# Where VectorE reads the decay sums and the queries in the recurrent heads, and the order of TensorE's work around two heads

## The reference, cut to what matters

```python
q, f_pre, i_v, g_o, u_a, u_b, gate_a, gate_b = jnp.split(proj, SPLITS, axis=-1)
logf = jax.nn.log_sigmoid(zf) + jnp.log1p(lb * jnp.exp(-zf))
k = (1.0 - lb) * jax.nn.sigmoid(-zf)
qh = heads(q) * (A_DK ** -0.5)
...
b = jnp.cumsum(logf, axis=2)
decay = jnp.exp(jnp.minimum(diff, 0.0)) * causal      # diff = b[t] - b[s]
attn = jnp.einsum('bhtd,bhsd,bhtsd->bhts', q, k, decay)
o = (jnp.einsum('bhts,bhsv->bhtv', attn, v)
     + jnp.einsum('bhtd,bhdv->bhtv', q * jnp.exp(b), S))
k_dec = k * jnp.exp(b_last - b)
```

## Time and profile before

| | |
|---|---|
| median of 3 runs | 852.73 us (850.11 to 853.77) |
| the profiled execution | 853.36 us |
| its span in the trace | 851.1 us |
| busy: TensorE | 811.1 us, 95% |
| VectorE | 405.9 us, 48% |
| ScalarE | 233.0 us, 27% |
| GpSimd | 141.5 us, 17% |
| bytes moved | 251.33 MB, mean 295 GB/s |

### The profile page before, as it was taken

One profiled execution on the slowest core, in us unless ns is written; L12 is line 12 of the kernel. 1 busy time (PEld: TensorE's weight loads), 2 busy tenths in 40 slices (PEclk: granted clock), 3 DMA queues, 4 the chain that ended last, 5 costly groups with the idle time before them and its releaser, 6 DMA issues.

```text
span 851.1 us, 12448 instructions
## 1 busy us (share of the span) xinstructions
PE 811.1 (95%) x5068; PEld 525.1 (62%) x5068; DVE 405.9 (48%) x682; ACT 233.0 (27%) x373; POOL 141.5 (17%) x170
## 2 busy tenths in 40 slices
PE   4999999999999999999999999999999999998892
PEld 2989999999999977585353533535335353352251
DVE  6789999988999723875011212112021120210127
ACT  6666655665444360111102010010000100000011
POOL 1354555433777200000000000000000000000000
PEclk9999999999999999999999999999999999999996
DMA  8422222344446453669999999999999999999971
GB/s 319 169 85 85 85 85 85 109 179 156 149 151 240 205 198 149 267 239 389 432 394 424 428 427 424 428 428 425 427 427 428 424 429 427 428 424 429 428 325 64
DMA packets 33894, 251.33 MB, mean 295 GB/s; under 512 B 4974, under 2 KB 8430, under 8 KB 21674
## 3 DMA queue, kind: packets, MB, share of 16 engines
q1 hardware_dynamic: 31296, 249.18, 71.8%
q10 hardware_dynamic: 2538, 1.32, 0.5%
HBM read 247.99 MB, written 2.48 MB: 294 GB/s over the span
## 4 chain that ended last, share of the span: by engine, by line
PE 69%; DVE 11%; DMA 9%; ACT 8%; issue 1%; ACTq 1%; DVEq 0%
PE ps L543 67%; DMA ring<-in_w_up_e 8%; DVE ring L1692 4%; ACT ring L1212 2%; ACT ar L1222 1%; DVE ar L1728 1%; ACT split_w L1131 1%; DVE ar L1739 1%; PE ps L940 1%; DVE ar L1683 1%; ACTq L1261 1%; ACT ar L1184 1%; DVE ring L1601 1%; DVE ar L1735 1%; ACT ar L1183 0%
## 5 line engine op out<-in xcount | busy, mean ns | idle before, releaser
L543 PE MATMUL ps<-ring,ar 128*64 128x512 f32 (+1 forms) x976 | 202.1, 567 | 1.6 <-DMA ring<-in_w_up_e 1.2
L543 PE MATMUL ps<-ring,xT 128*64 128x512 f32 (+2 forms) x848 | 151.0, 455 | 6.1 <-DMA ring<-in_w_gate_e 3.1
L543 PEld LDWEIGHTS ps<-ring,ar 128*64 128x64 f32 x976 | 67.9, 137 | 121.1 <-issue 111.8
L543 PEld LDWEIGHTS ps<-ring,xT 128*64 128x64 f32 (+1 forms) x848 | 75.5, 154 | 74.3 <-issue 63.8
L543 PE MATMUL ps<-split_x,split_t 128*128 128x320 f32 x672 | 99.2, 309 | 0.0
L543 PEld LDWEIGHTS ps<-split_x,split_t 128*128 128x128 f32 x672 | 98.6, 188 | 0.2
L2105 DVE TENSOR_TENSOR ar<-ar,ps 128x512 f32<-128x512 f32 (+1 forms) x42 | 28.7, 684 | 135.0 <-PE ps L543 134.3
L543 PE MATMUL ps<-split_x,split_w 128*128 128x320 f32 x480 | 79.8, 322 | 3.8 <-DVE split_w L1652 1.2
L543 PEld LDWEIGHTS ps<-split_x,split_w 128*128 128x128 f32 x480 | 73.2, 193 | 7.0 <-ACT split_x L1166 2.1
L1815 DVE SCALAR_TENSOR_TENSOR ps<-ar,params,ps 128x350 f32<-128x350 f32 x116 | 68.1, 587 | 4.1
L543 PE MATMUL ps<-ar 128*64 128x512 f32 (+7 forms) x424 | 66.8, 342 | 0.0
(11 more groups left out here) (232 smaller groups left out, 850.3 us busy)
## 6 DMA issues: line engine op xcount, KB each, us to landing
ring<-in_w_gate_e SPq DMA_DIRECT2D x29, 2048.0 KB, 21.8
ring<-in_w_up_e SPq DMA_DIRECT2D x29, 2048.0 KB, 18.6
ring<-in_w_down_e SPq DMA_DIRECT2D x22, 2048.0 KB, 18.1
ring<-in_w_in SPq DMA_DIRECT2D x56, 512.0 KB, 4.5
ar<-in_w_down_e SPq DMA_DIRECT2D x4, 1792.0 KB, 18.9
ring<-in_w_down_end SPq DMA_DIRECT2D x3, 2048.0 KB, 36.7
ar<-in_w_up_e SPq DMA_DIRECT2D x3, 1792.0 KB, 14.8
ring<-in_w_o_a SPq DMA_DIRECT2D x8, 512.0 KB, 5.8
```

Source lines behind the costliest of these rows:

```text
L543: return pe.matmul(out, lhsT, rhs, start=start, stop=stop)
```

## The change

VectorE's `level_decay` takes the running sum of its own columns from PSUM. Bank 0, where F(n) stood, is free by then, and a new ScalarE copy, `sum_copy`, puts `hb` there (semaphore `b_ps`). The middle value that is subtracted still comes from SBUF. `query_side` and the `hqeb` product take Q(n) straight from bank 1 in place of ScalarE's copy `hq`; the copy stays for the levels' diagonal. So QSCALE moves from that copy into the split weights: ScalarE's `w_high` scales the Q weights, VectorE's `w_low` becomes one scalar_tensor_tensor for Q. Since the banks are in use for longer, F waits for `dr_ready` (the decays of the head before) in place of `ls_ready`, and Q for `qeb_ready` in place of `q_sb`.

In TensorE's order the second head takes the levels of head 0 right behind F(1), ahead of the transposes and of Q(1). Behind the last head the levels of head 7 come right behind `conv_value(0)`, ahead of the router's matmul and `rms`.

```diff
             def cur_f(i, b, first):
...
-                    pe.wait_ge(h["ls_ready"], 2 * i + b)
+                    pe.wait_ge(h["dr_ready"], 2 * i + b)
...
             def cur_q(i, b, first):
...
-                    pe.wait_ge(h["q_sb"], 2 * i + b)
+                    pe.wait_ge(h["qeb_ready"], 2 * i + b)
...
-                if first or first_prev:
+                if first:
                     cur_q(*cur, first)
                 if first_prev:
+                    levels(*prev, True)
                     prev_kT(*prev, True)
-                    levels(*prev, True)
+                    cur_q(*cur, first)
                     prev_states(*prev)
...
-            pe.wait_ge(h["ls_ready"], 8)
+            pe.wait_ge(h["dr_ready"], 8)
             conv_value(0)
-            pe.wait_ge(h["q_sb"], 8)
+            levels(3, 1, False)
+            pe.wait_ge(h["qeb_ready"], 8)
             for k in range(KT):
                 mm(ps[:, 1, T:T + 2 * NE], ones, wgb[:, k, :], k == 0, k == KT - 1)
             rms(3, 0, 1)
-            levels(3, 1, False)
             prev_kT(3, 1, False)
...
-                signal(act, act.activation(piece(wh, q), sh[:, b, q].rearrange("p k n -> p (k n)"), ACT.Copy), whi_ready, 2 * n + q + 1)
+                signal(act, act.activation(piece(wh, q), sh[:, b, q].rearrange("p k n -> p (k n)"), ACT.Copy, scale=(1.0, QSCALE)[q]), whi_ready, 2 * n + q + 1)
...
-                signal(act, act.activation(hq[:, b, :], ps[:, 1, 0:T], ACT.Copy, scale=QSCALE), h["q_sb"], n + 1)
+                signal(act, act.activation(hq[:, b, :], ps[:, 1, 0:T], ACT.Copy), h["q_sb"], n + 1)
...
+            def sum_copy(i, b):
+
+                n = 2 * i + b
+                act.wait_ge(h["b_ready"], n + 1)
+                signal(act, act.activation(ps[:, 0, 0:T], hb, ACT.Copy), h["b_ps"], n + 1)
...
                 key_exp(*cur)
+                if first_prev:
+                    sum_copy(*cur)
                 if prev:
                     prev_states(*prev, first_prev)
+                if not first_prev:
+                    sum_copy(*cur)
                 if nxt:
                     w_high(*nxt, 0)
...
-                signal(dve, dve.tensor_tensor(piece(wl, q), sh[:, b, q].rearrange("p k n -> p (k n)"), piece(whF, q), ALU.subtract), wlo_ready, 2 * n + q + 1)
+                raw = sh[:, b, q].rearrange("p k n -> p (k n)")
+                ins = dve.scalar_tensor_tensor(piece(wl, q), raw, QSCALE, piece(whF, q), ALU.mult, ALU.subtract) if q else dve.tensor_tensor(piece(wl, q), raw, piece(whF, q), ALU.subtract)
+                signal(dve, ins, wlo_ready, 2 * n + q + 1)
...
             def level_decay(i, b):
...
+                dve.wait_ge(h["b_ps"], n + 1)
...
-                    ins = dve.tensor_tensor(xv[:, :, hs:2 * hs], bv[:, :, hs:2 * hs], bv[:, :, hs - 1:hs].to_broadcast([P, w // (2 * hs), hs]), ALU.subtract)
+                    here = ps[:, 0, 0:w].rearrange("p (m s) -> p m s", s=2 * hs)[:, :, hs:2 * hs]
+                    ins = dve.tensor_tensor(xv[:, :, hs:2 * hs], here, bv[:, :, hs - 1:hs].to_broadcast([P, w // (2 * hs), hs]), ALU.subtract)
...
-                    qv = hq[:, b, 0:w].rearrange("p (m s) -> p m s", s=2 * hs)[:, :, hs:2 * hs]
-                    ins = dve.tensor_tensor(xv, xv, qv, ALU.mult)
+                    qv = ps[:, 1, 0:w].rearrange("p (m s) -> p m s", s=2 * hs)[:, :, hs:2 * hs]
+                    ins = dve.tensor_tensor(xv, qv, xv, ALU.mult)
...
-                signal(dve, dve.tensor_tensor(hqeb, heb, hq[:, b, :], ALU.mult), h["qeb_ready"], n + 1)
+                signal(dve, dve.tensor_tensor(hqeb, ps[:, 1, 0:T], heb, ALU.mult), h["qeb_ready"], n + 1)
```

More of the change, by code:

```diff
@@ L269, in build @@
                  "kde_ready xr_ready xk_ready a_done am_ready as_ready qeb_ready kdec_ready kT_done kT_sb s_done sa_sb o_done "
-                 "osq_ready rms_done rstd_ready rstd_exp o_out so_ready so_stored hc_dve hp_dve hc_act hp_act hc_pool hp_pool fold_ready v_sb round")
+                 "osq_ready rms_done rstd_ready rstd_exp o_out so_ready so_stored hc_dve hp_dve hc_act hp_act hc_pool hp_pool fold_ready v_sb b_ps round")
         h = {n: sem(n) for n in names.split()}
```

## The result

The changed kernel takes 852.73 us (median of 20 runs, 850.96 to 855.85) against 850.99 (20 runs of the kernel before, 849.09 to 853.77): a ratio of 1.0022, 95% interval 1.0013 to 1.0031, 1.7 us slower. I had forecast 1.2 us faster. The size is inside the range and inside "within 0.5%", the direction is wrong. (The 20 runs put the kernel before at 850.99; the three that I had gave 852.73.) That 852.73 lies inside 849.0 to 854.5 says little for the working: the kernel before lies inside it too.

A forecast was written before the change was run, and what follows sets the result against it. In the steady heads a ScalarE-VectorE loop of 19.24 us was taken as the bound, TensorE 0.2 us behind. First heads +0.7, steady heads -0.98, last head -0.9 gave -1.2 us: 851.5 us, range 849.0 to 854.5.

The forecast's parts named there:

- The decays at 2.5: VectorE's seven decay subtractions in a steady head fall from 4.15 to 2.5 us with one input in PSUM.
- The ceiling of the steady heads: Five steady heads: TensorE's work, 19.06 us, replaces the 19.24 us ScalarE-VectorE loop; about 1 us gain at most.
- The 0.77 at the first `rms`: TensorE's lost 0.58 + 0.19 us up to the first `rms` vanishes, as ScalarE's chain there starts earlier.
- F-to-`rms` at 3.6: Sign of being right: TensorE goes from F's start to `rms` in 3.6 us in all heads.
- That it passes on: Behind the heads, VectorE's tap chain and TensorE both move by 1.2 us, and expert loads start 1.2 earlier.
- B: Rival: strided PSUM reads are slow, decays up to 6.0 us, 13 us more, 865; chance 0.07.
- C: Rival: VectorE and GpSimd still take turns, decays stay 4.15 and the five waits stay; 853.0, chance 0.08.
- The first heads: First two heads: TensorE idles 1.7 us before the levels, V is 1.5 late; net loss 0.7 us (0.5 to 1.2).
- GpSimd's key side speeds up only to about 3.8: Head 0: GpSimd's key side falls from 4.27 to about 3.8 us (bounds 3.6 and 4.27), ending at 41.1.
- The big exponential stays at 35.16: Head 0: ScalarE's big exponential keeps its start, released by GpSimd's decays of 3.63 us from 31.42.
- The last head: Behind the last head: levels moved ahead cover TensorE's wait for `rms`; gain 0.9 us.
- D: Rival: stages behind the heads shift VectorE's taps by 1 to 2 us, up to 853.5; chance 0.15 for over 1 us loss.

The follow-up runs named there:

- e5: The kernel before with only the two new TensorE orders (second head, last head), Q still waiting for `q_sb`; ratio 1.0003.
- e4: The changed kernel, but in head 0 VectorE's `w_low` waits until GpSimd's decays are done; ratio 0.9995.
- e3: The changed kernel with twelve extra unread matmuls into an unused bank ahead of the second head's levels; ratio 0.9995.
- e7: The kernel before with only the decays read from PSUM, and that from the second head on; head 0 reads SBUF without copy; ratio 0.9951.
- e2: The changed kernel with TensorE's old order behind the last head (router matmuls, `rms`, then levels); ratio 1.0009.
- e6: The kernel before with only `sum_copy`, F waiting for `dr_ready` and decays from PSUM in all heads; 848.90 us against 852.25, ratio 0.9952.
- e10: The same kernel as e7, run again against the kernel before; ratio 0.9966.
- e1: The changed kernel with TensorE's old order in the second head (F, Q, transposes, levels); ratio 1.0007.
- e8: The changed kernel with the old order behind the last head and head 0's `w_low` waiting for GpSimd's decays; ratio 0.9983.
- e9: The changed kernel with both old TensorE orders and head 0 as before (SBUF reads, no copy, Q(1) waiting for `q_sb`); ratio 0.9965.

## Why the prediction was wrong

**Right.** The decays at 2.5 (2.44). The ceiling of the steady heads: "TensorE sets the period at 19.06", gain 0.98; measured 18.99 and 1.28. The extra 0.06 a head is the `rms` matmuls themselves, which took 0.71 to the next start where they had been waited for (78.25 to 78.96) and take 0.63 now, less the 0.02 by which F-to-`rms` is over the 3.61 that I took. The 0.77 at the first `rms`: 0.81. F-to-`rms` at 3.6: 3.63. That it passes on, as far as the rows go: from the gates to the first expert matmul the two differ by 0.2 us, and +1.83 in the heads stands beside +1.74 between the medians; behind that matmul single executions scatter too much to tell. Rivals B and C are out: 324 ns an operation with an input in PSUM, at each stride. By the Trainium skill ("VectorE: DVE Perf Modes", the section on the TRN2 errata) a PSUM source has 62 fixed cycles more; the runs don't show that: `hqeb` with one input from PSUM (41.35 above) and the sum of two SBUF rows are both 0.49, the decays 0.324 and 0.33.

**Wrong, and it decides: the step "The first heads", with a loss of 0.7 us.** Place and releaser were right (TensorE idle ahead of the levels, GpSimd's key side the last). Every size was too small; measured from V(0) to V(1), 1.5 became 3.98. Since V(0) shifts, I take the shares from the start of VectorE's running sum of head 0 to V(1):

| kernel | sum starts | V(1) starts | between |
|---|---|---|---|
| before | 30.45 | 47.63 | 17.18 |
| e5 orders alone | 31.30 | 50.32 | 19.02 |
| e4 low part waits | 31.01 | 50.20 | 19.19 |
| e3 gap filled | 30.82 | 50.78 | 19.96 |
| changed | 30.66 | 51.82 | 21.16 |

- The order itself: I expected that filling less of the gap costs 1.5. By e5 it costs 1.84, with no read or wait changed in the heads.
- "GpSimd's key side speeds up only to about 3.8". It doesn't speed up: 4.40, and 4.24 to 4.58 in e4 to e7. Operations of 160 columns take 0.53 there (median) both before and after; I had taken the decays' 0.45 for it. The turns had cost VectorE time, 4.35 to 2.44, and GpSimd nearly none. VectorE's own gain doesn't help either, since the levels wait for the later of the two: from e5 to e4 the query side gets shorter, the key side 0.34 longer, and V(1) comes 0.17 later.
- "The big exponential stays at 35.16, because GpSimd's decays, 3.63 from 31.42, release it". They didn't stay 3.63. I shortened VectorE's decays and didn't ask what VectorE would start next to them: `w_low`, 1.22 us with two SBUF inputs, now began ahead of GpSimd's last operation and held it to 1.38. From e4 to e3 (both at full clock there) that costs 0.77: the decays are 0.93 longer, the key side 0.16 shorter in e3.
- The clock. I priced a gap of TensorE at its own length. Behind 3.29 us of idling levels and transposes ran at half clock: 1.20 from e3 to the changed kernel. No row of before has such a gap, so I had no term and no rival for it.

1.84 + 0.17 + 0.77 + 1.20 = 3.98.

**Wrong too: the step "The last head", a gain of 0.9 us.** It came to 0.06. The step saw the wait at `rms` and covered it, but what waits for `rms` is `conv_gate(0)`, by way of ScalarE's norm factor, and the levels had covered that. "Name what is late next" was not done here. The forecast total of 0.9 was to be had, without the reorder: 0.89 in e2 and e6 to e10 (21.66 to 20.77), all of it from the decays.

With these two, -0.7 for -1.2: the two gains that I had right (2.09 together) stand against 3.98. The rivals didn't hold the case either: D put a loss behind the heads, while it lay in them.

## What to carry to other kernels

A step that shortens one engine's work starts that engine's next instruction earlier: look at what that is, and whom it holds (here a 1.2 us operation with two SBUF inputs, started ahead of GpSimd's last piece, cost 2 us with the clock that fell behind the longer gap). Before moving a step out of a gap, write down what it covers on both sides; a wait covered by moving work is often only moved to the next consumer. And a gap of TensorE isn't always priced by its length alone (those of 2.3 and 3.3 us here were not): read the granted clock behind it.

## What was not expected of the hardware

- TensorE's granted clock fell to 0.50 in the second head in the three executions with a gap of 3.29, 3.29 and 2.30 us there (the changed kernel, e2, e1), and stayed at 1.00 behind 1.82 (e5) and 1.83 (e4 and e8), and in e3, where the gap was filled. In the changed kernel it fell within the gap, at 42.2, in e1 a microsecond after Q had started, at 43.3. How long it stayed down is not set by the gap: about 3.4 us in the changed kernel and twice that in e2, with the same 3.29. What decides either, no run here shows; each is one execution.
- VectorE, with two SBUF inputs, and GpSimd take turns in both directions, an operation at a time. By the Trainium skill ("SBUF — State Buffer", the section "SBUF: two separate sides") whichever starts first holds the pair for its whole instruction; the runs agree roughly: a GpSimd operation of 0.45 that started 0.15 behind a VectorE operation of 1.22 took 1.38 us, where waiting that one out would make 1.52, and all seven took 3.59 once they may start first (e4). VectorE's short operations in turn cost GpSimd little: 0.53 an operation of the key side with turns and 0.52 without, but 0.77 in place of 0.62 for the last one, beside the 0.49 product of `carry_side`.
- The profiled execution of the changed kernel has a second piece of half clock, near 387 us, where the kernel before has none. Other kernels have it or not with the same work: 3.4 us in e8 and e9, twice that in e2 and e3, where gates to first expert matmul is 212.4 in place of 210.5 to 210.8, and none in the other six. Six runs (e1, e3, e5 to e8) also have 10 us at half clock ahead of the heads, from 16 to 26 us. I read both as scatter; it wasn't tested.
